# Column quarters for norms and router, softmax ahead of the tokens' transposes, and a regrouped first block

## The chip, the cores and the metric

The kernel runs on one core of a Trainium2 chip. The metric is the device time of one execution in microseconds (us). TensorE (PE) multiplies, VectorE (DVE) and ScalarE (ACT) work elementwise, GpSimd (POOL) does a little, and SyncE (SP) starts the DMAs. All arithmetic is float32; a matmul of 128x128 weights by 512 columns stands in the trace as two records.

## The reference

Two blocks of two layers each on a sequence of 512 tokens and width 1024. The second block takes 256 context tokens beside them. Shortened:

```python
def first_block(x, mem, ...):
    for l in range(2):
        h = rms_norm(x, norm_mix_w[l])
        x = x + hybrid_mixer(h, ...)     # sliding window, "fox" (forgetting) attention, SSM of 16 heads; then w_out
        x = x + memory_cross_attention(rms_norm(x, ...), rms_norm(mem, ...), ...)
    return rms_norm(x, final_norm_w)

# forgetting attention: c = cumsum(log_f)
logits = q @ k * scale + c[query] - c[key]
# SSM: per head, y = (C B^T * decay) @ (x * dt) + C @ state * exp(acs)

def second_block(x, c, ctx, ...):
    for l in range(2):
        m = silu(c) @ w_mod[l] + b_mod[l]           # six shifts, scales and gates
        h = rmsnorm(x) * (1 + m[1]) + m[0]          # the context cx likewise
        x = x + m[2] * (token_mixers(h, hc, ...) @ w_out[l])
        x = x + m[5] * expert_choice_ffn(modulate(rmsnorm(x), m[3], m[4]), ...)
        # the context too in layer 0

def expert_choice_ffn(h, w_router, ...):            # 16 experts
    aff = softmax(h @ w_router)                     # over the experts
    vals, idx = top_k(aff.T, 2 * t // 16)           # 64 tokens (context: 32) for each expert
    ...                                             # gather, gated FFN, weighted scatter
```

## The kernel before, in words

Activations lie transposed: `x` and `h` are eight tiles of 128 channels by up to 768 columns (512 tokens `T`, then 256 of memory or context). Weights come as 748 "units" of 512 KB (`in_stream`) into a ring of eight slots, some into `y_sb`, `h_sb` and `work` during the experts. SP starts the DMA of a slot as soon as PE has counted up `w_turn` for the unit in it. Each engine's program is written out in order; the engines meet by semaphores. On PE `claim(b, who)` waits until bank b's last reader has freed it. Everything that follows stays in the order of the code, so an instruction that waits holds back all behind it on its engine.

- **Norms** (`sum_squares`, L1524): ACT squares two tiles at a time, PE multiplies eight tiles by a matrix of ones (128 columns wide), which leaves the sum on all partitions; ACT takes Ln and Exp (`deviations`), DVE multiplies (`norm`, `modulated`). There are eleven such sums of 512 columns and five of 256.
- **First layer** (`first_layer`, L1622 on PE, L1883 on ACT, L2012 on DVE): norm, ten projections, five multiplications by the rotation matrix `C_ROT1` with DVE work behind each (three operations of 128x512), then `attention` over sliding-window units with projections "beside". After the fifth unit DVE runs `decays`: gates, their cumulative sum, and the negated sum. Then fox attention: each of 16 units has for two halves the scores, two matmuls that add c of the query and take off c of the key (one operand is a broadcast 0/1 column), and the mask.
- **SSM** (from L1649 on PE): twelve convolved projections, transposes of `xbc` that ACT copies out, small matmuls that bring gates and sums to tokens (`tok`), six state products, then the loop over 16 heads. Per head: `broadcast_sums` (bank hh % 2), ACT exponential `e_off`, DVE four `tensor_scalar` of 128 columns, ACT exponential of `diff`, DVE four `scalar_tensor_tensor` (`m_dec`, with the head's dt) and one `tensor_tensor` (`c_off`), PE seven matmuls with 64-column weights (`xs_tok`, `prev`). `pair_out` is two DVE operations per pair of heads.
- **Modulation beside the heads**: three of 48 units per head (`mod_unit`, eight matmuls with 32-column weights in four column groups), 12 groups copied out by ACT, and `mod_columns`: four matmuls of 128x128 weights by 2 columns for each group.
- **Output and memory attention** (L1719 on): projections in two halves with norms between.
- **Second block** (`pe_second`, `act_second`, `dve_second`): norms, projections, grid attention, gated recurrence, output, norm, `experts`.
- **experts**: PE waits for all tiles of `h`, multiplies tokens by the router weights (weights: 128x128 of `h`, 16 columns moving, 48 matmuls with the context), transposes the tokens (12 groups of 4, ACT copies), DVE starts the softmax, ACT's Exp stands behind its twelve copies. Then DVE `choose`: eight rounds of `max` and `match_replace` on 512 columns, and in layer 0 four rounds on 256; a scan gives ranks, PE turns them, DVE builds one-hot matrices, PE gathers.

## Time and profile before

| | us |
|---|---|
| median of 3 runs (lowest to highest) | 3955.86 (3952.66 to 3958.94) |
| the profiled execution's own time | 3957.54 |
| its span in the trace | 3955.8 |
| busy: PE, DVE, ACT, POOL | 3695.8, 1177.2, 909.4, 142.1 |
| HBM read | 404.49 MB, 103 GB/s over the span |

The span is the time from the first to the last instruction of the execution; its own time lies 1.7 us above. Busy time of an engine says little by itself: what matters is which wait ends last in each stage. "PEclk" is the TensorE clock that was granted, as a share of 2.4 GHz; its two levels are 1.0 (2.4 GHz) and 0.5 (1.2 GHz).

### The profile page before, as it was taken

The page shows a single profiled execution, that of the slowest core. Times are in us where ns is not written, and L with a number is a line of the kernel's source. Part 1 is how long each engine was busy: PE and PEld are TensorE (multiplying, and loading weights), DVE is VectorE, ACT ScalarE, POOL GpSimd, SP SyncE. Part 2 cuts the span into 40 slices and gives each one's busy share as a digit, 9 for nine tenths or more (in the row PEclk, how much of TensorE's full clock was granted, in tenths as well). Part 3 has the DMA queues.
Part 4 walks back from the last instruction along what each step waited for, and adds up shares of the span by engine and source line. Part 5 has one row for each costly group of instructions (what it writes and reads, how often), then busy time and mean ns, then how long its engine had stood idle before and what let it go on. Part 6 is the DMA issues. An engine that isn't in the chain of part 4 may idle for free.

```text
span 3955.8 us, 46968 instructions
## 1 busy us (share of the span) xinstructions
PE 3695.8 (93%) x19856; PEld 2170.5 (55%) x19856; DVE 1177.2 (30%) x2568; ACT 909.4 (23%) x1710; POOL 142.1 (4%) x162
## 2 busy tenths in 40 slices
PE   8999899999999899999999889879999999787999
PEld 4555464754465464755756566654434656554553
DVE  1322441021322441022433584120002333752011
ACT  1343220111343220113224220211112233311110
POOL 0000000000000000000000340000000000320000
PEclk9999999999999999999999999889999999887999
DMA  3111261311111271312100001137762110012897
GB/s 141 59 49 48 74 246 64 114 47 64 54 53 47 69 253 64 112 40 92 38 27 33 1 2 56 62 128 281 288 255 86 38 43 22 1 49 101 318 345 278
DMA packets 113104, 409.63 MB, mean 104 GB/s; under 512 B 12289, under 2 KB 14465, under 8 KB 112513
## 3 DMA queue, kind: packets, MB, share of 16 engines
q1 hardware_dynamic: 112896, 406.63, 28.5%
q8 instruction: 159, 2.61, 0.3%
q14 instruction: 49, 0.39, 0.0%
HBM read 404.49 MB, written 2.10 MB: 103 GB/s over the span
## 4 chain that ended last, share of the span: by engine, by line
PE 88%; DVE 8%; ACT 2%; issue 1%; DMA 1%; POOL 0%; DVEq 0%; SPq 0%; ACTq 0%
PE bank L1487 85%; PE bank L1594 1%; DVE work L1275 0%; DMA ring<-in_stream 0%; ACT work L1822 0%; DVE h_sb L2117 0%; DVE work L1345 0%; DVE work L1973 0%; ACT h_sb L892 0%; DVE work L1975 0%; DVE ring L1249 0%; DVE small L1344 0%; DVE levels L1275 0%; DVE ring L1248 0%; PE bank L1655 0%
## 5 line engine op out<-in xcount | busy, mean ns | idle before, releaser
L1487 PE MATMUL bank<-h_sb,ring 128*128 128x512 f32 (+1 forms) x3152 | 1234.9, 545 | 14.9 <-DVE y_sb L1149 4.6
L1487 PEld LDWEIGHTS bank<-h_sb,ring 128*128 128x128 f32 x3152 | 588.4, 191 | 549.7 <-issue 518.4
L1487 PE MATMUL bank<-y_sb,ring 128*128 128x512 f32 (+1 forms) x1152 | 476.2, 576 | 14.1 <-DVEq L196 9.7
L1487 PE MATMUL bank<-work 128*128 128x128 f32 (+5 forms) x3168 | 438.2, 317 | 46.8 <-DVEq L196 15.3
L1487 PEld LDWEIGHTS bank<-work 128*128 128x128 f32 (+2 forms) x3168 | 325.5, 178 | 132.1 <-issue 84.4
L1487 PEld LDWEIGHTS bank<-y_sb,ring 128*128 128x128 f32 x1152 | 220.6, 192 | 265.7 <-issue 247.9
L1487 PE MATMUL bank<-ring,h_sb 128*128 128x128 f32 (+3 forms) x2304 | 317.0, 314 | 18.7 <-ACTq L196 17.2
L1788 ACT ACTIVATE work<-bank 128x512 f32<-128x512 f32 (+1 forms) x275 | 140.2, 525 | 804.0 <-PE bank L1487 634.2
L1487 PEld LDWEIGHTS bank<-ring,h_sb 128*128 128x128 f32 (+2 forms) x2304 | 266.0, 195 | 60.5 <-issue 39.2
L1487 PE MATMUL bank<-ring,work 128*64 128x512 f32 (+1 forms) x800 | 209.3, 596 | 0.8 <-DMA ring<-in_stream 0.8
L1487 PE MATMUL bank<-y_sb,work 128*64 128x128 f32 (+2 forms) x920 | 168.7, 430 | 0.0
L1487 PE MATMUL bank<-work,y_sb 128*128 128x512 f32 (+1 forms) x496 | 137.8, 436 | 13.1 <-DVE ring L1249 6.6
L1799 ACT ACTIVATE h_sb<-x_sb 128x1024 f32<-128x1024 f32 (+1 forms) x56 | 48.0, 896 | 434.5 <-DVEq L196 428.6
L1788 ACT ACTIVATE y_sb<-bank 128x512 f32<-128x512 f32 (+1 forms) x163 | 86.9, 555 | 194.2 <-PE bank L1487 183.2
L1985 DVE TENSOR_REDUCE small<-bank 128x1 f32<-128x256 f32 (+3 forms) x96 | 41.7, 465 | 287.4 <-PE bank L1487 287.2
L1452 POOL MEMSET work<- 128x1024 f32 x4 | 3.7, 951 | 3194.6 <-ACTq L196 3194.6
L1487 PE MATMUL bank<-h_sb,const 128*128 128x512 f32 (+1 forms) x262 | 104.7, 556 | 14.0 <-ACT h_sb L1799 6.0
L1487 PEld LDWEIGHTS bank<-ring,work 128*64 128x64 f32 (+1 forms) x800 | 57.5, 128 | 96.8 <-issue 96.7
L1487 PEld LDWEIGHTS bank<-work,y_sb 128*128 128x128 f32 (+1 forms) x496 | 59.3, 169 | 85.4 <-issue 61.8
L1822 ACT ACTIVATE work<-work,small 128x256 f32<-128x256 f32 (+3 forms) x124 | 73.1, 590 | 128.2 <-DVEq L196 128.1
L1487 PE MATMUL bank<-ring 64*128 64x128 f32 x840 | 78.9, 331 | 23.8 <-DVE work L1275 15.1
L1594 PEld LDWEIGHTS bank<-const,work 128*128 128x128 f32 x576 | 69.0, 141 | 57.0 <-issue 39.4
(274 smaller groups left out, 3543.6 us busy)
## 6 DMA issues: line engine op xcount, KB each, us to landing
ring<-in_stream SPq DMA_DIRECT2D x578, 512.0 KB, 4.4
y_sb<-in_stream SPq DMA_DIRECT2D x110, 512.0 KB, 6.2
h_sb<-in_stream SPq DMA_DIRECT2D x40, 512.0 KB, 8.0
work<-in_stream SPq DMA_DIRECT2D x20, 512.0 KB, 9.7
work<-in_bias SPq DMA_DIRECT2D x2, 2688.0 KB, 9.4
x_sb<-in_xT SPq DMA_DIRECT2D x4, 512.0 KB, 6.1
out<-x_sb SPq DMA_DIRECT2D x8, 256.0 KB, 2.0
const<-in_consts SPq DMA_DIRECT2D x1, 1058.0 KB, 15.8
```

Source lines behind the costliest of these rows:

```text
L1452: ins = V.memset(level_sums[d][n], 0.0)
L1487: return nc.tensor.matmul(o, a, b, start=first, stop=last, skip_group_check=True)
L1594: ins = nc.tensor.transpose(banks[b][:, j * P:(j + 1) * P], scores_in(i - 1, s)[:, kb * P:(kb + 1) * P], ident)
L1788: me.link(A(o, i, func, **kw), freed_by_act, wait=False)
L1799: me.link(A(dst[:, k:k + 2, :], src[:, k:k + 2, :], ACT.Square), squares_ready, wait=False)
L1822: me.link(A(at, banks[s][:, 0:u["nk"]] if raw else at, ACT.Exp, bias=nmax[:, j:j + 1], scale=1.0 if raw else -1.0, accum_out=rsum[:, j:j + ...
L1985: me.link(V.reduce_max(m, banks[s][:, 0:nk], AX.X, negate=True), max_ready, wait=False)
```

## The change

1. Sums of squares: weights of 32 columns of ones, tile k in column group k % 4 (`quarter_squares`), so that four partial sums stand on four groups of 32 partitions. ACT copies them (`quarters`), one more matmul by the full matrix of ones adds them (`add_quarters`), and the scale divides by 32. In the out and memory stages these calls stand between projections.
2. Router: the router's weights (32 columns of the slot) are stationary, `h` moves, in column quarters, each tile as soon as it is ready. ACT copies the parts, six (four) matmuls with `C_EXPERTS` add them token-major. The tokens' transposes are split into groups 0-1, 2-5 and 6-11, around softmax and choosing; ACT's Exp comes after two copies.
3. Choosing: context experts lie on partitions 32 to 47 beside the grid's on 0 to 15, in one `[48, 512]` table filled with -1, so four of the eight rounds choose for both.
4. First layer: the five rotations stand among the projections (banks 4 and 5).
5. Fox: c of the query and of the key are added by one matmul instead of two. `decays` makes the tables for it: two copies, two memsets and four `tensor_scalar` of 128x512 more.
6. SSM: gates and sums go to tokens first; DVE copies `xs_tok` out and multiplies by dt there, `m_dec` becomes one `tensor_tensor` of 512 columns. Three banks for `broadcast_sums`, four buffers for `m_dec` and `c_off`, heads in pairs whose matmuls alternate between the two column halves.
7. Modulation: `mod_columns` (48 matmuls per layer) gives way to `add_mod_rows` (12 matmuls by 512 columns, weights of 32 columns) and four transposes after the output projections' first half.

```diff
-            def sum_squares(b, tile, n, k_tiles=KT, what=C_ONES):
-                claim(b, None)
-                for k in range(k_tiles):
+            def quarter_squares(b, tile, n):
+                claim(b, "act")
+                for k in range(KT):
                     if k % 2 == 0:
                         pe.wait_ge(squares_ready, me.nth(squares_ready))
-                    ins = mm(banks[b][:, 0:n], cst(what), tile(k), k == 0, k == k_tiles - 1)
+                    at = slice(32 * (k % 4), 32 * (k % 4) + 32)
+                    ins = mm(banks[b][at, 0:n], cst(C_ONES, 32), tile(k), k < 4, k >= 4)
                 ins.then_inc(full_for_act, 1)
+            def add_quarters(b, n, at=0):
+                pe.wait_ge(quarters_ready, me.nth(quarters_ready))
+                claim(b, None)
+                mm(banks[b][:, 0:n], cst(C_ONES), quarter_sums[:, at:at + n], True, True).then_inc(full_for_act, 1)
... ACT
+            def quarters(b, n, at=0):
+                bank_full()
+                me.link(A(quarter_sums[:, at:at + n], banks[b][:, 0:n], ACT.Copy), freed_by_act)
+                me.notify(quarters_ready)
... PE, experts
-                for j in range(n_tok):
-                    for k in range(KT):
-                        ins = mm(banks[0][:, j * 16:j * 16 + 16], h[:, k, j * P:(j + 1) * P], w[:, k, 0:16],
-                                 k == 0, k == KT - 1)
+                for s in range(1 + both):
+                    claim(s, "act")
+                    for k in range(KT):
+                        tile_ready()
+                        of = slice(32 * (k % 4), 32 * (k % 4) + 32)
+                        ins = mm(banks[s][of, 0:(T, CTX)[s]], w[:, k, 0:32], h[:, k, SPANS[s]], k < 4, k >= 4)
+                    ins.then_inc(full_for_act, 1)
+                turn_tokens(range(2))
+                pe.wait_ge(freed_by_act, parts_read)
+                claim(2, "dve")
+                for j in range(n_tok):
+                    ins = mm(banks[2][:, j * 16:j * 16 + 16], logit_parts[:, j * P:(j + 1) * P], cst(C_EXPERTS, 16), True, True)
+                ins.then_inc(full_for_dve, 1)
+                turn_tokens(range(2, 6))
... DVE, choose
-                for s, cap in enumerate((CAP, CAP_CTX)[:1 + both]):
-                    for _ in range(cap // 8):
-                        me.link(V.max(top8, left[:, SPANS[s]]))
-                        me.link(V.match_replace(left[:, SPANS[s]], top8, left[:, SPANS[s]], -1.0))
+                for n in range(CAP // 8):
+                    rows = slice(0, 48 if both and n < CAP_CTX // 8 else 16)
+                    me.link(V.max(top8[rows, :], left[rows, :]))
+                    me.link(V.match_replace(left[rows, :], top8[rows, :], left[rows, :], -1.0))
... PE, first_layer
+                    if 2 <= n < 7:
+                        pe.wait_ge(freed_by_act, projected[n - 2])
+                        claim(4 + n % 2, "dve")
+                        mm(banks[4 + n % 2][:, :], cst(C_ROT1), flat((n - 2) * T, T), True, True).then_inc(full_for_dve, 1)
... PE, head loop, modulation
-                def mod_columns(g):
-                    pe.wait_ge(mod_rows_ready, me.nth(mod_rows_ready))
-                    for n in range(4):
-                        ins = mm(banks[7][:, 8 * g + 2 * n:8 * g + 2 * n + 2], mod_rows[:, g % 2, n * P:(n + 1) * P],
-                                 cst(C_PICK, 2), True, True)
+                def add_mod_rows(q):
+                    for _ in range(4):
+                        pe.wait_ge(mod_rows_ready, me.nth(mod_rows_ready))
+                    for j in range(4):
+                        ins = mm(banks[7][32 * j:32 * j + 32, :], cst(C_PICK + 4 - 2 * q, 32), mod_rows[j], q == 0, q == 2)
... fox_units
-                                 (half, 0, n, one.to_broadcast([64, P]), negc[r, 0:n]),
-                                 (half, 0, n, c[r, qi], one.to_broadcast([64, n]))]
+                                 (half, 0, n, decay_of[t][r, qi], decay_keys[r, 0:n])]
... DVE, decays
+                        me.link(V.tensor_copy(decay_all[of_queries, :], decay_all[rows, :]))
+                        me.link(V.memset(decay_all[rows, :], 1.0))
+                    for t in range(4):
+                        me.link(V.tensor_scalar(decay_of[t], decay_all, const[:, C_DECAY + t:C_DECAY + t + 1], None, ALU.mult))
... PE, heads
+                for t in range(HEADS // 2):
+                    for n in range(PER_PAIR):
+                        mod_unit(PER_PAIR * t + n)
+                    for half in range(2):
+                        pe.wait_ge(operand_ready, me.nth(operand_ready))
+                        broadcast_sums(2 * t + half + 3)
...
+                    for c in range(CHUNKS):
+                        for earlier in range(1 + (c > 0)):
+                            for hh in (2 * t, 2 * t + 1):
+                                rows = slice(hh % 2 * 64, hh % 2 * 64 + 64)
...
+                                if earlier:
+                                    ins = mm(banks[b][rows, cs], prev[:, c - 1, hs], c_off[hh % 4][:, cs], False, True)
+                                else:
+                                    ins = mm(banks[b][rows, cs], xs_tok[:, c, hs], m_dec[hh % 4][:, cs], True, c == 0)
...
+                add_mod_rows(2)
... DVE, tokens of the SSM (ACT's copies of xs_tok are gone)
+                for c in range(CHUNKS):
+                    for g in range(2):
+                        bank_full()
+                        me.link(V.tensor_tensor(by_head(xs_tok[:, c, g * T:(g + 1) * T]), by_head(banks[(2 * c + g) % 4][:, :]),
+                                                per_head(tok, c, g), ALU.mult), freed_by_dve, wait=False)
... DVE, heads
-                    for c in range(CHUNKS):
-                        cs = slice(c * P, (c + 1) * P)
-                        me.link(V.scalar_tensor_tensor(out=m_dec[:, r, cs], in0=diff[:, r, cs],
-                                                       scalar=tok[:, c * 16 + hh:c * 16 + hh + 1], in1=cbm[:, g, cs],
-                                                       op0=ALU.mult, op1=ALU.mult), wait=False)
+                    me.link(V.tensor_tensor(m_dec[hh % 4], diff[:, r, :], cbm[:, g, :], ALU.mult), wait=False)
+                    if hh >= 3 and r:
+                        pair_out((hh - 3) // 2)
```

How the order moves, at three places. PE, the norm and the choosing of layer 0 of the second block, from the last output projection to the first gather (`const,h_sb` are the tokens' transposes, `work 128x128` the gather). Before:

```order
L1487 MATMUL bank<-y_sb,ring 128x256 x8
L1487 MATMUL bank<-h_sb,const 128x512 x8
L1487 MATMUL bank<-h_sb,const 128x256 x8
L1487 MATMUL bank<-ring,h_sb 128x16 x48
L649 MATMUL bank<-const,h_sb 128x128 x48
L656 MATMUL bank<-const,small 16x128 x6
L1487 MATMUL bank<-const,work 128x16 x6
L1487 MATMUL bank<-work 128x128 x80
```

Now:

```order
L1518 MATMUL bank<-h_sb,const 32x512 x8
L1518 MATMUL bank<-h_sb,const 32x256 x8
L1518 MATMUL bank<-work,const 128x512
L1518 MATMUL bank<-work,const 128x256
L1518 MATMUL bank<-h_sb,ring 32x512 x8
L1518 MATMUL bank<-h_sb,ring 32x256 x8
L661 MATMUL bank<-const,h_sb 128x128 x8
L1518 MATMUL bank<-const,work 128x16 x6
L661 MATMUL bank<-const,h_sb 128x128 x16
L1518 MATMUL bank<-const,small 16x128 x4
L1518 MATMUL bank<-const,small 32x128 x2
L661 MATMUL bank<-const,h_sb 128x128 x24
```

48 router matmuls of 16 columns became 16 of 512 or 256 columns and six small ones, and 24 of the 48 transposes now come behind the turned affinities.

PE, two heads of the SSM (`ring,cond` modulation units, `work,const` broadcast sums, 64x128 the heads' products). Before, one head, and then the next begins alike:

```order
L1487 MATMUL bank<-work,const 128x512
L1487 MATMUL bank<-const,h_sb 128x2 x4
L1487 MATMUL bank<-ring,cond 32x128 x24
L1487 MATMUL bank<-work 64x128 x2
L1487 MATMUL bank<-work,h_sb 64x128
```

Now, the first pair:

```order
L1518 MATMUL bank<-work,const 128x512 x3
L1518 MATMUL bank<-ring,cond 32x128 x48
L1518 MATMUL bank<-work,const 128x512 x2
L1518 MATMUL bank<-work 64x128 x4
L1518 MATMUL bank<-work,h_sb 64x128 x2
L1518 MATMUL bank<-work 64x128 x2
```

The pair's products stand together, after both heads' operands.

DVE, `decays` between two sliding-window units, now:

```order
L2096 SCALAR_TENSOR_TENSOR work<-work 8x512
L2098 SCALAR_TENSOR_TENSOR work<-work 8x512
L2100 TENSOR_SCALAR work<-work 8x512
L2102 COPY work<-work 8x512
L2103 MEMSET work 8x512
L2105 TENSOR_SCALAR work<-work,const 128x512 x2
L2105 TENSOR_SCALAR levels<-work,const 128x512 x2
L2106 SCALAR_TENSOR_TENSOR work<-work 16x512
```

The first five rows stand twice (rows 0 to 7 and 64 to 71); copy, memset and the four rows of L2105 are new, before the next unit's mask.

## Rows read from the trace of the kernel before

**Rows 1.** Page: busy us of each engine (share of the span); ACT's costliest group, copies

```profile
PE 3695.8 (93%) x19856; PEld 2170.5 (55%) x19856; DVE 1177.2 (30%) x2568; ACT 909.4 (23%) x1710; POOL 142.1 (4%) x162
...
L1788 ACT ACTIVATE work<-bank 128x512 f32<-128x512 f32 (+1 forms) x275 | 140.2, 525 | 804.0 <-PE bank L1487 634.2
```

**Rows 2.** Timeline (start, us, engine, operation, [idle before]): choosing, layers 0 and 1

```profile
2540.99 20.63 PE L1487 MATMUL bank<-ring,h_sb 128*128 128x16 f32 x96 [9.36 <-ACTq L196]
...
2561.46 8.29 PE L649 MATMUL bank<-const,h_sb 128*128 128x128 f32 x48
...
2570.48 0.33 ACT L989 ACTIVATE small<-small 128x96 f32<-128x96 f32 x1
...
2574.12 0.68 DVE L1344 MAX8 small<-work 16x8 f32<-16x512 f32 x1
...
2586.05 0.42 DVE L1344 MAX8 small<-work 16x8 f32<-16x256 f32 x1
...
2593.43 2.73 PE L1487 MATMUL bank<-const,work 16*128 16x16 f32 x12 [20.94 <-DVE work L1351]
...
2598.22 19.64 PE L1487 MATMUL bank<-work 128*128 128x128 f32 x160 [2.06 <-issue]
...
3614.27 13.81 PE L1487 MATMUL bank<-ring,h_sb 128*128 128x16 f32 x64 [7.87 <-ACTq L196]
...
3655.25 16.59 PE L1487 MATMUL bank<-work 128*128 128x128 f32 x128 [1.70 <-issue]
```

**Rows 3.** Timeline: a norm between output projections; PE groups: column-quartered matmuls, all

```profile
594.02 7.03 PE L1487 MATMUL bank<-h_sb,const 128*128 128x512 f32 x16
...
603.28 9.23 PE L1487 MATMUL bank<-y_sb,ring 128*128 128x512 f32 x17 [2.23 <-DVE y_sb L1951]
...
L1487 PE MATMUL bank<-ring,cond 128*32 128x128 f32 x1536 | 49.8, 279 | 0.0
```

**Rows 4.** Stretches (rotations; router): us, busy PE PEld DVE ACT POOL; PEclk; DMA; GB/s

```profile
88.50:101.40 12.90, 4.58 (x12) 1.84 (x12) 10.38 (x15) 1.99 (x3) 0.00 (x0) 0.79 0.00 0
...
2545.00:2555.00 10.00, 10.00 (x48) 10.00 (x49) 0.00 (x0) 0.00 (x0) 0.00 (x0) 0.50 0.73 294
```

**Rows 5.** Heads of the SSM: stretches, timeline, and PE matmuls alternating between column halves

```profile
506.00:559.00 53.00, 48.87 (x697) 37.28 (x698) 35.48 (x101) 16.05 (x28) 0.00 (x0) 1.00 0.85 302
...
1819.00:1822.00 3.00, 2.95 (x7) 1.43 (x8) 2.96 (x6) 3.00 (x6) 0.00 (x0) 1.00 1.03 416
...
507.34 0.38 PE L1487 MATMUL bank<-work,h_sb 128*64 128x128 f32 x2
...
507.65 1.12 PE L1487 MATMUL bank<-work,const 16*128 16x512 f32 x2
...
511.40 1.14 DVE L2126 SCALAR_TENSOR_TENSOR work<-h_sb,small,cpad 128x128 f32<-128x128 f32 x4 [0.77 <-ACT h_sb L1910]
...
512.46 0.68 DVE L2129 TENSOR_TENSOR work<-work,h_sb 128x512 f32<-128x512 f32 x1
...
514.66 1.13 DVE L2117 TENSOR_SCALAR h_sb<-bank,small 128x128 f32<-128x128 f32 x4 [1.52 <-ACT h_sb L1908]
...
L1487 PE MATMUL bank<-y_sb,work 128*64 128x128 f32 x480 | 32.6, 279 | 0.0
```

**Rows 6.** PE groups: matmuls that add c, 0/1 operand stationary; timeline: decays and behind it

```profile
L1487 PE MATMUL bank<-const,work 64*128 64x512 f32 x32 | 8.2, 590 | 0.0
...
L1487 PE MATMUL bank<-const,work 64*128 64x384 f32 x32 | 6.5, 483 | 0.0
...
L1487 PE MATMUL bank<-const,work 64*128 64x256 f32 x32 | 4.8, 377 | 0.0
...
L1487 PE MATMUL bank<-const,work 64*128 64x128 f32 x32 | 3.2, 272 | 0.0
...
159.97 0.48 DVE L2039 TENSOR_SCALAR work<-work,small 16x512 f32<-16x512 f32 x1
...
163.59 0.70 PE L1487 MATMUL bank<-work 64*128 64x256 f32 x4 [1.61 <-DVE small L1980]
```

More of the change, by code:

```diff
@@ L489, in build @@
         hidden_t = [v.rearrange("p (k s) -> p k s", k=4) for v in (rstd[:, 0:512], flat(12032, 512), acc_o[:, 0:512])]
-        aff_t, left, ranks = (work[0:16, 8960 + n * ALL:8960 + (n + 1) * ALL] for n in range(3))
+        logit_parts = flat(7424, ALL)
+        left, ranks = (work[0:48, at:at + T] for at in (9728, 10496))
+        CTX_ROWS = slice(32, 48)
         gathered = [[v.rearrange("p (e k s) -> p e k s", e=2, k=KT) for v in pair]
@@ L1324, in choose @@
             def choose(both):
+                me.link(V.memset(left, -1.0))
                 bank_full()
```

292 lines of the change are left out of this document (156 added, 136 removed).

## The prediction

> **What bounds the kernel now.** I read the page first. TensorE is busy for 3695.8 of the 3955.8 us of the span [rows 1]; the other engines are far below. So the change can save in two ways: less TensorE work where TensorE never rests, and shorter waits in the few stretches where it rests. Then I cut the span into stages and read the timeline where TensorE was idle. The largest such place is the choosing of experts: from the router's first matmul to the first gather it takes 57.2 us in layer 0 and 41.0 us in layer 1 [rows 2]. Others are the rotations, where TensorE works 4.6 of 12.9 us [rows 4], and the norms. In the heads of the SSM TensorE works 48.9 of 53.0 us (five pairs of heads, 10.6 each) while the DMA engines stand at 0.85 and 302 GB/s [rows 5]: two resources close together.
>
> **The change, part by part.** A matmul of 128x128 weights and 512 columns takes 0.88 us (7.03 / 8) [rows 3]. Eight column-quartered ones of 128 columns take 0.52 us: 49.8 us over 96 units [rows 3]. One whole matmul of 128 columns would be a quarter of 0.88, 0.22 us, and eight 1.76 us; so quartering gains a factor 3.4, and eight quartered matmuls by 512 columns cost 8 x 0.88 / 3.4 = 2.1 us.
>
> 1. *Covered norms* (out and memory stages; per layer two of 512 columns, one of 256). Where the first now stands between projections it cost 594.02 to 603.28 = 9.3 us [rows 3], the waits for Ln, Exp and VectorE included. After: 2.1 + 0.9, and the wait lies under the next projection: saves 6.3. The second of 512 saves 7.0 - 3.0 = 4.0, the one of 256 half of it, 2.0. Four transposes for the modulation cost 4 x 0.17 (8.29 / 48 [rows 2]) = 0.7. Per layer 11.6, and about 1.5 for a low clock that no longer follows the rest, an estimate: 13 us; twice, **26**.
> 2. *Norms on the path* (start of each first layer, the first block's final norm, four of the second block). TensorE waits anyway. What counts is the chain behind the last squares: before the rest of eight matmuls, now the last pair (0.5), ACT's copy (0.6 with its start; 0.53 in the mean [rows 1]), one matmul (0.9). Each saves 1.5 to 5 us, the more where 256 columns follow 512. But TensorE idles longer before it begins again, and behind a rest its clock is at the 1.2 GHz level: 0.79 in the mean over the rotations, 0.50 in the router [rows 4]. I take **17** for the seven, between 7 and 25.
> 3. *Rotations.* TensorE's 4.4 us (five by 0.88) stay, now among projections, and the stretch of 12.9 us goes [rows 4]; VectorE's 10.4 us are hidden by projections of 7 us each. Saved 8.5, and some 2.3 because the window units no longer begin at the low clock: 10.8 per layer, **21.6**.
> 4. *Fox.* One of two equal matmuls goes: 8.2 + 6.5 + 4.8 + 3.2 = 22.7 us over both layers [rows 6]. TensorE does not rest in this stage, so all of it is saved: **22.7**.
> 5. *Its price, `decays`.* VectorE gets four operations of 128x512 and four of 8x512 between two window units, at about 0.48 each [rows 6] and with gaps 4.1 us. Behind them waits the next unit's mask, and for that the scores of the unit after on TensorE, which already wait 1.61 us for it [rows 6]; nothing is left to hide more. Per layer -4.1 and -0.9 for the clock: **-10** (between -4 and -14).
> 6. *SSM, before the heads.* Gates to tokens first, then the transposes, whose copies (now VectorE's, 0.68 as `c_off` [rows 5] instead of 0.53) end later: **-2** in all.
> 7. *Heads.* TensorE per pair now: two sums by 512 columns at 1.1 [rows 5], six units at 0.52 = 3.1, fourteen products at 0.136 (32.6 / 240 [rows 5]) = 1.9, together 7.2 us instead of 10.6. VectorE per head: four `tensor_scalar` 1.13, a wait for ScalarE 0.77, `m_dec` 0.68, `c_off` 0.68 [rows 5], 3.3; per pair with `pair_out`, two more of 128x512, 8.1 us. So VectorE sets the pace: 2.5 us less per pair, 20 per layer. The DMA must bring six units, 3.15 MB, per pair: 7.6 us at the 416 GB/s seen elsewhere [rows 5], 8.9 at the 355 that 302 GB/s at a share of 0.85 would make; eight units lie in the ring beforehand. For a DMA nearly as slow I take 17 per layer: **34** (between 12 and 42).
> 8. *Choosing, layer 0.* The router's matmuls (20.6 us) ride on the tiles as they come, 0.5 behind the last; the transposes (8.3) no longer stand before Exp [rows 2]. The path then: 0.5; two copies 1.1; six small matmuls at 0.43 (20.63 / 48) = 2.6; max and subtraction 0.6; from Exp to the first round 3.6 (2570.48 to 2574.12), and 1.0 more because four groups of transposes stand before the turned affinities; eight rounds 11.9 (2574.12 to 2586.05); of the 7.4 up to 2593.43 four context rounds (3.8) and a third of the rest's columns go, 2.5 stay; 4.8 from there to the gather [rows 2]. Sum 28.6 instead of 57.2: **28.6**. That a round on 48 partitions lasts as long as on 16 I assume from the operations of 8x512, 16x512 and 128x512, which hardly differ.
> 9. *Choosing, layer 1.* The same with four token tiles: 0.5 + 0.6 + 1.7 + 0.5 + 3.4 + 1.0 + 11.9 + 2.4 + 3.6 = 25.6 instead of 41.0: **15.4**.
>
> The expert passes stay as they are: twelve units beside the ring's eight are fetched while choosing goes on, 15 us at 416 GB/s. Sum: 26 + 17 + 21.6 + 22.7 - 10 - 2 + 34 + 28.6 + 15.4 = 153.3 us. The profiled execution took 3957.5 us, 1.7 above the median; 3957.5 - 153.3 = **3804**, some 3802 beside a median run.
>
> A rule speaks against parts 1, 7 and 8. Between the start of the last 64-column product (507.34) and that of the next full-width matmul (507.65) lie 0.31 us [rows 5], where products follow each other at 0.22: a change of width costs about 0.1 us, with some 50 such changes added 5 us in all, inside the range. The Trainium skill (TensorEngine Tiling (Array Packing), Tiling Modes, Key Properties) says that a change of tiling mode drains TensorE, and gives no figure; a costly drain would join the second rival.
>
> **The rivals.**
> - *The heads stay as slow as they are*, held by the DMA or by ScalarE's turns. For it: share 0.85, and ScalarE's copies of the modulation between two exponentials. Against: 416 GB/s elsewhere. Part 7 gives 0: 3804 + 34 = 3838.
> - *Quarters do not overlap when 512 columns move.* Then eight cost 7 us again: eleven norms lose 5 us, five 2.5, the routers 13: about 80, so 3884. Against: the factor 3.4 in rows 3, though with 128 columns.
> - *Softmax is not ahead*: Exp or the parts wait behind something else, and half of what parts 8 and 9 promise is lost: 3826.
> - *Slower than before: the clock.* In the router TensorE was busy all the time and yet at 1.2 GHz [rows 4], with matmuls of 16 columns. If the new, lighter mix in heads and norms leaves the clock there and it does not come back in the projections behind, each us of TensorE work at full clock costs one more; it decides from 153 us of such work on. Heads at half clock, 14.4 us per pair instead of 10.6, are 30 more per layer and 17 not saved: 3804 + 94 = 3898. To be slower than before, a further 60 us of projections must run low: from there 4000 and more. The Trainium skill (TensorE: Matmul & The Clock Gate, What's actually happening) says that the throttled state is the default and activity releases it; by that rule the projections bring the clock back.
>
> **How the numbers follow.** Forecast 0.78; heads 0.09; softmax 0.06; quarters 0.04; clock 0.015; other 0.015. The bounds of parts 2, 5 and 7 add up to -36 and +22; not all at once, so 3782 to 3830 for the likeliest case alone. The range takes in the first and third rival: 3775 to 3848. A measurement can tell 0.2%, 8 us, from no change. All cases but the clock lie far below 3948: faster 0.98, same 0.005, slower 0.015.
>
> **What would show it.** In the new profile: some 29 and 26 us from the last router tile to the gather; the head loop at 8.1 us per pair with waits for VectorE; the stretch of 12.9 us gone; a wait of about 5 us on TensorE behind `decays`; column-quartered sums at about 0.26 us each. Wrong if quartered matmuls by 512 columns stand 0.88 apart, if the head loop keeps 10.6, or if the expert passes get longer because their weights come late.

## The result, and the profile after

| | before | changed |
|---|---|---|
| median of 4 runs (lowest to highest), us | 3954.26 (3949.38 to 3958.94) | 3824.52 (3820.65 to 3825.18) |
| the profiled execution: own time, span | 3957.54, 3955.8 | 3824.45, 3821.3 |

The ratio is 0.967, 95% interval 0.9653 to 0.9687. The forecast was 3804, range 3775 to 3848: the range holds the time, the point is 20 us too low. In a later group of runs the changed kernel gave 3821.21 (4 runs), ratio 0.9653 (0.9639 to 0.9666). The interval of every ratio below is about as wide, 5 us to either side; the difference of two runs carries both intervals and is uncertain by some 7 us. A difference smaller than that is read from the traces, stage by stage, or not at all. One of the five executions of experiment 2 took 5180.22 us at a granted clock of 0.67 and is left out of what follows, while all others of a version agree within 0.4%.

The page of the changed kernel, busy times, against [rows 1]:

```profile
PE 3581.4 (94%) x19542; PEld 2060.3 (54%) x19542; DVE 1179.8 (31%) x2497; ACT 911.5 (24%) x1715; POOL 142.1 (4%) x162
```

TensorE is busy for 114.4 us less and the span fell by 134.5, so 20 us of the gain is idle time of TensorE that went. Choosing in layer 0 and a covered norm, PE's timeline (start, duration, engine, line, operation, idle before), against [rows 2, 3]:

```profile
549.80 1.92 PE L1518 MATMUL bank<-h_sb,const 128*32 128x512 f32 x16
551.66 7.13 PE L1518 MATMUL bank<-y_sb,ring 128*128 128x512 f32 x16
558.63 1.02 PE L1518 MATMUL bank<-work,const 128*128 128x512 f32 x2
...
2447.38 8.40 PE L1518 MATMUL bank<-h_sb,ring 128*32 128x512 f32 x32 [2.55 <-ACT h_sb L920]
2455.71 1.09 PE L661 MATMUL bank<-const,h_sb 128*128 128x128 f32 x8
2456.64 1.41 PE L1518 MATMUL bank<-const,work 128*128 128x16 f32 x12
...
2476.68 2.74 PE L1518 MATMUL bank<-const,work 48*128 48x16 f32 x12 [12.89 <-DVE work L1382]
...
2481.49 1.83 PE L1518 MATMUL bank<-work 128*128 128x128 f32 x7 [2.06 <-issue]
```

Eight quartered matmuls by 512 columns last 1.92 us instead of 7.03, and a projection stands between them and the matmul that adds the quarters. From the router's first matmul to the gather it is 34.1 us (2447.38 to 2481.49). The router's 8.40 us of it now run while the tiles of `h` are still being made: the last tile is ready at 2455.06, and from there to the gather it is 26.4 us, where the forecast had 28.6. The window units behind `decays`, same view, against [rows 6]:

```profile
152.97 0.44 PE L1518 MATMUL bank<-work 128*64 128x128 f32 x4
159.31 1.23 PE L1518 MATMUL bank<-work 64*128 64x256 f32 x4 [5.90 <-DVE small L2043]
160.47 5.38 PE L1518 MATMUL bank<-h_sb,ring 128*128 128x512 f32 x8
```

The wait grew from 1.61 to 5.90 us. The eight records behind it (half a projection) take 5.38 us at a mean granted clock of 0.68. The same eight took as long in the kernel before, behind the shorter wait, while in experiment 3 (below), which has that shorter wait too, they take 3.70 (the kernel before, then experiment 3):

```profile
164.22 5.40 PE L1487 MATMUL bank<-h_sb,ring 128*128 128x512 f32 x8
```

```profile
152.97 0.70 PE L1520 MATMUL bank<-work 64*128 64x256 f32 x4 [1.61 <-DVE small L2045]
153.60 3.70 PE L1520 MATMUL bank<-h_sb,ring 128*128 128x512 f32 x8
```

The heads of both layers (us, busy PE, PEld, DVE, ACT, POOL, granted clock, DMA share, GB/s), then VectorE's timeline, against [rows 5]:

```profile
466.60:535.90 69.30, 61.99 (x1050) 41.55 (x1049) 51.20 (x115) 24.98 (x44) 0.00 (x0) 0.90 0.90 341
1315.90:1388.20 72.30, 64.39 (x1050) 42.99 (x1049) 50.96 (x114) 25.01 (x44) 0.00 (x0) 0.87 0.87 332
```

```profile
504.75 1.13 DVE L2193 TENSOR_SCALAR h_sb<-bank,small 128x128 f32<-128x128 f32 x4
...
508.68 0.69 DVE L2186 TENSOR_TENSOR y_sb<-y_sb,work 128x512 f32<-128x512 f32 x1
...
511.23 0.69 DVE L2197 TENSOR_TENSOR work<-h_sb,cpad 128x512 f32<-128x512 f32 x1 [0.69 <-ACT h_sb L1968]
...
512.56 1.13 DVE L2193 TENSOR_SCALAR h_sb<-bank,small 128x128 f32<-128x128 f32 x4
```

VectorE begins the same operation of the next pair 7.81 us later (504.75, 512.56); the forecast said 8.1.

Lengths of the stages, in us per layer (layer 0, layer 1), between the same instructions in each trace. Fox and the rest of the layer came out within 0.1 us of these values in every profile of the same code. The other stages vary from one profile to the next although their code is the same: projections, window units and the stage before the heads by 2 to 3 us, the heads by 5, the second block's body by 3 to 6. So a difference of one or two us in those is read from the mean of several profiles:

| stage (from, to) | before | changed |
|---|---|---|
| projections and rotations (first projection, first mask of the window units) | 85.2, 85.2 | 77.8, 76.6 |
| window units (to the first maximum of the fox units) | 151.7, 151.9 | 154.7, 154.5 |
| fox (to the memset of `cpad`) | 113.9, 113.9 | 105.5, 105.5 |
| convolution, SSM before the heads (to the first broadcast sum) | 110.0, 110.0 | 110.7, 112.9 |
| heads (to the first out projection) | 88.1, 84.9 | 69.3, 72.3 |
| rest of the first-block layer (to the end of its last projection) | 336.0, 336.0 | 323.5, 323.5 |
| second block, its unchanged body (first projection to the last out projection) | 702.3, 561.5 | 705.0, 566.5 |

### The profile page after: what moved, and what is told of

Its sections match the earlier page's. It is cut to its first block, busy times and chain, and to the rows that moved or that the text cites. A ratio compares the mean times of both kernels' runs of the same rounds, so it can differ in the third digit from the quotient of the medians.

```text
span 3821.3 us, 46294 instructions
## 1 busy us (share of the span) xinstructions
PE 3581.4 (94%) x19542; PEld 2060.3 (54%) x19542; DVE 1179.8 (31%) x2497; ACT 911.5 (24%) x1715; POOL 142.1 (4%) x162
## 4 chain that ended last, share of the span: by engine, by line
PE 86%; DVE 8%; ACT 2%; issue 1%; DMA 1%; POOL 0%; DVEq 0%; SPq 0%; ACTq 0%
PE bank L1518 84%; PE bank L1633 1%; DMA ring<-in_stream 1%; DVE work L1307 1%; DVE h_sb L2193 0%; ACT work L1880 0%; DVE ring L1281 0%; DVE work L2036 0%; DVE work L2038 0%; DVE levels L1307 0%; DVE work L1377 0%; PE bank L1705 0%; DVE cpad L1271 0%; DVE small L1376 0%; DVE ring L1280 0%
## 5 line engine op out<-in xcount | busy, mean ns | idle before, releaser
L1518 PE MATMUL bank<-h_sb,ring 128*128 128x512 f32 (+2 forms) x3200 | 1251.2, 548 | 25.1 <-ACT h_sb L920 13.4
L1518 PEld LDWEIGHTS bank<-h_sb,ring 128*128 128x128 f32 (+1 forms) x3200 | 594.2, 191 | 570.0 <-issue 529.3
L1518 PE MATMUL bank<-work 128*128 128x128 f32 (+7 forms) x3168 | 426.2, 322 | 29.8 <-DVE small L2043 12.2
L1518 PEld LDWEIGHTS bank<-work 128*128 128x128 f32 (+2 forms) x3168 | 317.5, 180 | 123.4 <-issue 85.9
L1518 PE MATMUL bank<-ring,h_sb 128*128 128x128 f32 (+2 forms) x2144 | 283.1, 310 | 1.4 <-ACT work L1033 0.7
L1518 PEld LDWEIGHTS bank<-ring,h_sb 128*128 128x128 f32 (+2 forms) x2144 | 231.9, 185 | 43.7 <-issue 40.9
L1518 PEld LDWEIGHTS bank<-work,y_sb 128*128 128x128 f32 (+1 forms) x496 | 59.6, 171 | 85.2 <-issue 61.8
L1633 PEld LDWEIGHTS bank<-const,work 128*128 128x128 f32 x576 | 69.2, 141 | 56.8 <-issue 40.1
L1518 PEld LDWEIGHTS bank<-y_sb,work 128*64 128x64 f32 (+1 forms) x920 | 61.6, 132 | 68.2 <-issue 63.5
```

The source lines that it names most:

```text
L1518: return nc.tensor.matmul(o, a, b, start=first, stop=last, skip_group_check=True)
L1633: ins = nc.tensor.transpose(banks[b][:, j * P:(j + 1) * P], scores_in(i - 1, s)[:, kb * P:(kb + 1) * P], ident)
```

## The experiments

All are edits of the changed kernel; 4, 10 and 11 make two or three at once. Each group of runs had its own runs of the kernel before: 1, 2, 3 and 5 (median before 3959.02); 6, 7 and 8 with a repeated run of the changed kernel (3959.46); 4, 9, 10 and 11 (3956.29). A "slower" or "shorter" below is against the changed kernel, 3824.52 or 3821.21, if nothing else is named.

**1. The burst of `decays` spread.**

```diff
-                    if between is not None and i == 5:
-                        between()
+                    if between is not None and i in (5, 6, 7, 8):
+                        next(between)
```

`decays` becomes a generator that yields behind each of its two gate blocks and behind the four `tensor_scalar`.

> The work of decays is the same, but VectorE does it in four portions behind the window units 5, 6, 7 and 8 and not in one burst of 12.3 us behind unit 5. Theory A (the forecast's part 5: the burst is what TensorE waits for, 5.9 us in the changed kernel's profile, and the low clock after it): each portion is at most 3.7 us and a unit's slack covers most of it, so the wait falls to under 2 us and the low clock after it goes; 3 to 5 us a layer, time 3815 to 3818. Theory B (VectorE has no slack in the window units: the work costs what it lasts wherever it stands): four waits of 1 to 2 us instead of one, time 3822 to 3826.

Measured: 3799.11 (3796.89 to 3805.43), ratio 0.9599 (0.9586 to 0.9612): more than either theory said. PE's timeline at the same place, and the whole window stage:

```profile
153.99 1.07 PE L1518 MATMUL bank<-work 128*64 128x128 f32 x8
154.99 3.70 PE L1518 MATMUL bank<-h_sb,ring 128*128 128x512 f32 x8
```

```profile
96.82:243.35 146.53, 145.63 (x704) 84.11 (x704) 43.24 (x154) 54.29 (x142) 0.00 (x0) 1.00 0.18 62
```

No wait is left and the clock stays at 1.00. The stage is 146.5 us in both layers, 8.1 less than in the changed kernel, twice the expectation: the whole wait and the low clock went, where I had let a part of each stay. So theory A holds, though its time (3815 to 3818) was missed. The two stages are 16.1 us together and the profile is 19.2 shorter; the rest of the 22 to 25 us of the medians lies inside their intervals.

**2. Rotations behind the projections again** (part 3 undone): the five matmuls by `C_ROT1` after `all_read("act")`, on banks 0 to 3.

> The changed kernel with the five rotations back behind the projections (part 3 undone), all else kept. Theory A (part 3 as forecast: 8.5 us for the stretch and 2.3 for the clock of the window units): slower by 21.6, 3846. Theory B (part of that gain was eaten, as the lengths of the stages in the two profiles say: projections and rotations 6.55 us shorter in layer 0 and 7.8 in layer 1): slower by 14 to 15, 3839. In both, TensorE idles some 8 us a layer again behind the last projection.

Measured: 3842.42 (median of four), ratio 0.9705 (0.9691 to 0.9718), 18 to 21 us slower. Its timeline has the old gap:

```profile
86.71 4.56 PE L1518 MATMUL bank<-work,const 128*128 128x512 f32 x10 [0.69 <-ACT y_sb L1840]
98.93 0.80 PE L1518 MATMUL bank<-work 64*128 64x128 f32 x4 [7.67 <-DVEq L199]
```

The stages up to the fox units are 6.6 us longer in layer 0 and 11.9 in layer 1 (84.8 + 154.3 and 87.6 + 155.4). That is 18.5 by the two profiles, and 19.9 against the mean of the seven profiles that share the changed kernel's code up to the fox units (231.1 a layer). It lies between the theories, 21.6 and 14 to 15, nearer to A. That the rotations behind the projections cost the gap is shown; how much of the clock's part belongs to it isn't.

**3. Two decay products again, no tables** (parts 4 and 5 undone).

```diff
-                                 (half, 0, n, decay_of[t][r, qi], decay_keys[r, 0:n])]
+                                 (half, 0, n, one.to_broadcast([64, P]), decay_keys[r, 0:n]),
+                                 (half, 0, n, decay_all[r, qi], one.to_broadcast([64, n]))]
```

> The changed kernel with the two decay products per fox unit back and without the prepared tables (parts 4 and 5 undone). Theory A (forecast: one product is worth 22.7 us over both layers, its preparation costs 10): slower by 12.7, 3837, the fox stage of a layer 11.35 longer and the window stage 5.0 shorter. Theory B (the stage lengths of the two profiles: fox 8.65 in layer 0): the fox stage only 8 to 9 longer, because something else now bounds it a little; the sum slower by 12 to 13 as well, since the window stage loses 2.4.

Measured: 3826.55, ratio 0.9665 (0.9652 to 0.9678), no slower than the changed kernel within the interval. Both theories missed. The fox stage is 113.92 us, so the product is worth 8.4 a layer; the window stage is 148.4, so the tables cost 6.2 of the 154.6; parts 4 and 5 together bring 4.5 us over both layers, not 12.7.

**4. Two decay products, and `decays` spread** (the smaller work of experiment 3 in the four slots of experiment 1).

> The changed kernel with decays spread over four units and with two decay products per fox unit instead of one (no prepared tables). Theory A (one product is worth 8.65 us a layer, as the fox stage shows when it is put back, and the preparation of the tables costs nothing once spread): slower by 17 than the spread version alone, 3816. Theory B (spreading helped by something else than the tables' time): 3799 to 3806 with the smaller work in decays.

Measured: 3817.57, ratio 0.9647 (0.9633 to 0.966). Window stage 146.75, fox stage 113.9. Beside experiment 1 that is 0.2 and 8.4 longer: spread, the tables cost nothing, and the single product keeps all of its 16.9 us. The run is 18.5 us slower than experiment 1, from another group, where theory A said 17.

**5. Sums of squares whole again, at the new places.**

```diff
-                    ins = mm(banks[b][at, 0:n], cst(C_ONES, 32), tile(k), k < 4, k >= 4)
+                    ins = mm(banks[b][:, 0:n], cst(C_ONES), tile(k), k == 0, k == KT - 1)
```

The copy and the added matmul are gone too, and for the last sum of a layer ACT's Ln stands one copy earlier.

> The changed kernel with every sum of squares by eight matmuls of full width again, at the new places in the program, and without the copy and the added matmul (the quartering of parts 1 and 2 undone, their placement kept). Theory A (quarters overlap as forecast, factor 3.4): the covered norms lose 4.0 us for 512 columns and 2.0 for 256, 20 in all, and the seven on the path 1.5 to 5 each, about 17: slower by 30 to 40, 3855 to 3865. Theory B (what helped was the placement; quartered matmuls by 512 columns stand 0.88 apart or the copy and the added matmul give the gain back): within 5 us of 3824.

Measured: 3841.50, ratio 0.9703 (0.969 to 0.9717), 17 to 20 slower: outside both theories, whose bounds were 30 to 40 and 5. PE's timeline:

```profile
547.54 7.03 PE L1518 MATMUL bank<-h_sb,const 128*128 128x512 f32 x16
554.40 13.90 PE L1518 MATMUL bank<-y_sb,ring 128*128 128x512 f32 x32
```

The rest of a first-block layer is 333.4 us, 9.9 longer than with quarters and 2.6 shorter than before: of part 1's 12.5 us a layer the quarters give 9.9, the new places 2.6. On the path, TensorE's gap before the next weights' matmul grows from 7.16 to 9.10 (start of layer 1), 22.20 to 25.73 (final norm and first norm of the second block), 8.53 to 11.94 and 7.98 to 9.85 (behind the second output projections), 81.28 to 83.89 (expert sums and norm of layer 1): 13.4 us. That is 33 in all in the stages that the edit touches, theory A's figure, but the run is only 19.6 longer by its profile. Stages that it doesn't touch were shorter: the second block's body in layer 0 took 699.9 instead of 705.0 us, the heads 5.1 less in both layers together, projections and window units 3.3. Each of these stages varies between profiles of the same code, and here all are at or near their short end; that this is chance isn't shown.

**6. Only half of each modulation unit loaded.** The second half of a unit's room keeps what lay there.

> The changed kernel with only the first half (512 of 1024 columns) of each of the 96 modulation units loaded; the second half of a unit's room keeps what lay there, so the modulation vectors are not those of the reference. Nothing else differs, TensorE does the same matmuls. Theory A (the heads of the SSM are bound by the transfers, in layer 1 more than in layer 0: 0.84 share with four waits for landings there, 0.97 share in layer 0): layer 1's heads from 74.7 us to some 66, layer 0's from 69.1 to 65 or 66, time 3811 to 3815. Theory B (VectorE's turns, 8.1 us a pair, and ScalarE's copies set the pace, the transfers are only close by): 0 to 3 us less, 3821 to 3824.

The changed kernel repeated beside it, which gave 3821.21:

> The changed kernel itself once more, unaltered, as the point from which the other runs of this group are read: 3824 within 0.2% (3817 to 3832).

Measured: 3812.29, ratio 0.9634 (0.9621 to 0.9647).

```profile
465.80:533.50 67.70, 61.50 (x1050) 42.51 (x1049) 51.16 (x115) 25.11 (x44) 0.00 (x0) 0.90 0.61 196
1308.80:1376.50 67.70, 61.50 (x1050) 42.57 (x1049) 51.18 (x115) 25.11 (x44) 0.00 (x0) 0.90 0.62 201
```

The heads take 67.7 us in both layers. In the nine profiles that share the changed kernel's head loop and loads they took 67.5 to 72.3, 70.0 in the mean of 18. So with all transfers the heads are 2.3 us a layer longer on average, and 4.6 in layer 1 of the first profile (69.2 in the repeated run). Of those 4.6, TensorE waited 1.6 directly for landings; its busy time was 2.9 longer, 64.39 against 61.50, at a granted clock of 0.87 instead of 0.90, and whether the transfers brought that isn't shown. The time lies in theory A's range, but the heads of both layers together hold only some 5 of the 8.9 us by which the run is shorter than the repeated one, where A had 12 in the heads: theory A in kind, between the two in size. The rest lies in stages that the edit doesn't touch. (The expectation counts layer 1's heads from 2.4 us earlier than the table, 74.7 for 72.3.)

**7. Eight modulation units ahead of the heads,** one before and between each of the six state products, on banks 5 and 6; five instead of six units a pair are left.

```diff
-        PER_PAIR, MOD_GROUPS = 6, 12
+        MOD_AHEAD, PER_PAIR, MOD_GROUPS = 8, 5, 12
...
+                        mod_unit(2 * c + g + 1)
                         pe.wait_ge(operand_ready, me.nth(operand_ready))
                         claim(1 + g, "dve")
```

> The changed kernel with 8 of the 48 modulation units of a layer computed ahead of the heads, between the state products, where no transfer runs (share 0.00 over 24 us) and TensorE rests 4.4 us; five units a pair are left instead of six, so 32 units instead of 40 must land during the heads. Theory A (transfers bind the heads): layer 1's heads 8 to 10 us shorter, layer 0's 3 to 8, the stage before 0 to 2 longer per layer: 3808 to 3816. Theory B (VectorE and ScalarE set the pace): the heads stay at 65 us or more, and the 4.2 us of matmuls in the stage before cost up to 2 to 3 per layer: 3824 to 3830.

Measured: 3812.06, ratio 0.963 (0.9617 to 0.9644), inside theory A's range. The loads now run in the stage before (DMA share 0.52, 173 GB/s, where it was 0.00):

```profile
466.60:533.10 66.50, 56.58 (x924) 38.74 (x920) 50.61 (x113) 24.74 (x44) 0.00 (x0) 0.92 0.87 315
1309.60:1377.40 67.80, 57.98 (x925) 39.69 (x921) 50.60 (x114) 24.77 (x44) 0.00 (x0) 0.90 0.88 314
447.50:466.60 19.10, 17.82 (x192) 11.29 (x190) 16.11 (x25) 2.68 (x4) 0.00 (x0) 0.95 0.52 173
```

TensorE has 5.4 and 6.4 us less to do in the heads than in the changed kernel's first profile, and they are only 2.7 and 4.4 shorter, less than theory A said, and above 65 us as theory B said: something else sets their floor. Against the mean of the nine profiles the heads are 5.6 us shorter in both layers together, and the stage before them, which now holds the eight units, is 1.3 longer (111.8 and 111.0 against a mean of 110.7). So 4.3 of the 9.2 us of the medians are seen in the stages that the edit touches.

**8. Tokens' transposes all first** (the order of parts 8 and 9 undone).

> The changed kernel with all transposes of the tokens ahead of the logits and of the softmax, as before (the order of parts 8 and 9 undone), all else kept. Theory A (forecast: the transposes then stand on the path to the ranks): 40 more transposes of 0.17 in layer 0 and 24 in layer 1 ahead of the logits, 6.9 and 4.1, less the 1.0 each that the groups now stand ahead of the turned affinities, and Exp behind their copies: slower by 9 to 11, 3834. Theory B (the gain of parts 8 and 9 came from the router's matmuls alone, and the transposes were hidden either way): within 3 us, 3824.

Measured: 3828.84, ratio 0.967 (0.9657 to 0.9683), 7.6 slower than the repeated run.

```profile
2447.87 5.46 PE L661 MATMUL bank<-const,h_sb 128*128 128x128 f32 x48
2453.17 1.41 PE L1515 MATMUL bank<-const,work 128*128 128x16 f32 x12
```

Router to gather takes 39.2 us instead of 34.1 in layer 0 and 31.6 instead of 29.0 in layer 1. Theory A's mechanism, but 7.7 us where it had 9 to 11, since a transpose lasts 0.11 us here (5.46 / 48) and not the 0.17 of [rows 2], at the full clock instead of the low one.

**9. The context's rounds apart.** The rounds of the context's experts stand for themselves again: four `max` and `match_replace` rounds on rows 32 to 47 behind the grid's eight. I wrote them over the table's full 512 columns, not the 256 that the expectation names.

> The changed kernel with the context's experts chosen in rounds of their own behind the grid's (the part of 8 on the 48 partitions undone; layer 0 alone has a context). Theory A (forecast: a round on 48 partitions lasts as long as on 16, so the four context rounds of 256 columns are saved whole): 3.8 us longer from router to gather in layer 0, time 3825. Theory B (48 partitions made the grid's rounds longer, or the ranks wait for the transposes anyway): under 1 us longer, 3821 to 3822.

Measured: 3828.09, ratio 0.9668 (0.9655 to 0.9682), 4 to 7 slower. VectorE's rounds last 0.69 + 0.08 + 0.67 on 48 partitions and 0.68 + 0.08 + 0.66 on 16 in the changed kernel, so the assumption of part 8 holds. Between the first `max` and the ranks' matmul lie 20.4 us instead of 14.4: four rounds of 1.5.

**10. Spread `decays` and eight units ahead, together.**

> The two edits that made the changed kernel faster, together: decays in four portions and 8 modulation units ahead of the heads. Theory A (the stall behind decays and the transfers in the heads are separate losses, in other stages): the gains add up, 9 from the units ahead and 17 to 22 from the spread decays, from 3821 to 3790 to 3795. Theory B (both only moved the same DMA-bound or low-clock time): the second adds under 4 us, 3797 or more.

Measured: 3797.60 (3797.39 to 3802.62), ratio 0.9599 (0.9585 to 0.9612): the fastest median, 0.6% below the changed kernel. It misses theory A's range by 3 us and lies in theory B's, though not for B's reason: the two edits act in different stages. The window units take 146.5 us in both layers, the whole gain of experiment 1, and beside experiment 7 the profile is 17.5 us shorter. It is the units ahead that bring little. The heads take 67.8 and 68.1, 4.0 less than the mean of the nine profiles in both layers together, but the stage before them takes 111.9 and 112.3, 2.7 more than its mean: 1.3 us are left, and the medians of experiments 1 and 10, from different groups, differ by 1.5 (their ratios not at all). This profile is 6.2 us shorter than experiment 1's, but 2.0 of that is an earlier first projection, 2.8 the heads and the stage before them, and the rest lies in stages that neither edit touches.

**11. The same, with the product of each pair's output with its gate left out.**

```diff
-                    me.link(V.tensor_tensor(y[:, 8 + t, :], y[:, 8 + t, :], gtmp, ALU.mult))
```

> Decays spread and 8 modulation units ahead, and in the heads VectorE's product of each pair's output with its gate (one operation of 128x512 a pair) left out, so that the SSM's half of y holds the gates alone. Theory A (with the transfers out of the way VectorE's turns set the pace of the heads, as the forecast's part 7 has it): 0.68 us less a pair, 5 to 6 a layer, 10 to 12 below the version with the gate: 3781 to 3784. Theory B (TensorE or ScalarE's row copies set the pace): 0 to 3 us less, 3789 to 3794.

Measured: 3798.90 (3789.23 to 3799.18), ratio 0.9593 (0.9578 to 0.9609): the time can't tell it from experiment 10. The heads can: 63.4 and 64.3 us instead of 67.8 and 68.1.

```profile
494.46 1.13 DVE L2203 TENSOR_SCALAR h_sb<-bank,small 128x128 f32<-128x128 f32 x4
...
501.54 1.13 DVE L2203 TENSOR_SCALAR h_sb<-bank,small 128x128 f32<-128x128 f32 x4
```

A pair takes 7.08 us instead of 7.81, 0.73 less, as VectorE lost one operation of 0.69. So VectorE's turns with ScalarE set the pace of such a pair; per layer 4 of the 5.8 us come through. The gain is hidden in the sum: the first projection began 0.9 us later in this run, the projections of both layers took 4.0 more (77.7 twice, against 74.9 and 76.6), and the second block's body took 4.3 more in layer 0 (706.1 against 701.8).

## Why the prediction was right, and where 20 us went

The time came out inside the range, and the waits and overlaps that the parts name are found in the traces. But the point was 20 us off in a range 73 wide: two sizes were worked out wrongly (parts 4 and 2), and about half of the miss lies in stages that the forecast left at nothing. The parts, forecast and by the stages of the two profiles, split by an experiment where one separates them:

| part | forecast | measured | from |
|---|---|---|---|
| 1 covered norms | 26 | 25.0 | rest of the layer, 2 x 12.5 |
| 2 norms on the path | 17 | 14.4 | TensorE's gaps: -0.4, 1.9, 3.5, 3.2, 4.3, 1.9; the 3.2 and the last by when the last tile of `h` is ready |
| 3 rotations | 21.6 | 24.3 | experiment 3 against before, up to the fox units |
| 4 fox | 22.7 | 16.9 | 2 x (113.91 - 105.48) |
| 5 `decays` | -10 | -12.3 | window stages of the changed kernel against experiment 3 |
| 6 before the heads | -2 | -3.6 | stage table |
| 7 heads | 34 | 31.5 | 18.9 + 12.6 |
| 8 choosing, layer 0 | 28.6 | 31.2 | end of the out projections to the gather, 77.1 - 42.7, less 3.2 of part 2 |
| 9 choosing, layer 1 | 15.4 | 16.8 | the same, less 1.9 |
| unchanged second block; first projections; the rest | 0 | -9.7 | 705.0 - 702.3, 566.5 - 561.5; 1.7 against experiment 3; 0.3 |
| sum | 153.3 | 134.5 | the spans: 134.5 |

That the sum fits the spans says nothing for the split, since the stages cover the whole span. No run undid parts 6 and 7. What the pairs of heads, the single operation for `m_dec` and `add_mod_rows` each brought isn't shown.

**Part 3** came out 2.7 above its point. The projections are 8.8 us a layer shorter (76.3 and 76.4 in experiment 3, 85.2 before), the window units 3.3; of these, 1.7 is the half projection behind `decays`, 5.40 before and 3.70 in experiment 3. Undone alone, with the burst of `decays` in place, the part is worth only 18.5 to 19.9 (experiment 2), which suggests that its clock's share depends on what else holds TensorE up in the stage.

**Part 4** failed in its working. I read the worth of one product as the busy time of its groups [rows 6]. Busy time runs to the end of the last matmul, which overlaps the next group. What counts is the distance between starts. The trace of before, PE's timeline in one fox unit:

```profile
270.86 1.13 PE L1487 MATMUL bank<-work 64*128 64x512 f32 x4
271.82 1.02 PE L1487 MATMUL bank<-work,const 64*128 64x512 f32 x4
272.68 1.03 PE L1487 MATMUL bank<-const,work 64*128 64x512 f32 x4
273.64 0.71 PE L1487 MATMUL bank<-const 128*128 128x128 f32 x4
```

The second row lasts 1.02 us and the third starts 0.86 behind it. The other three sizes stand at 0.64, 0.43 and 0.22 (264.59 to 265.23, 258.58 to 259.01, 279.29 to 279.51); a unit of each is 2.15 us, and four of each are 8.6 a layer. Experiments 3 and 4 found 8.4. The reading was open to me before the prediction.

**Part 5** named the right place and the right wait. Its bounds (-4 to -14) hold the result near their end. The wait grew by 4.3 us in layer 0 and 4.6 in layer 1, where I had 4.1; the low clock behind it costs 2.2 and 1.6 against experiment 3, where I had 0.9. Against the kernel before, that low clock is nothing new, as its row of 5.40 shows: the table books it as gained in part 3 and lost again in part 5. And the statement "nothing is left to hide more" was true only of the place: experiment 1 shows that the same work costs nothing once no unit carries more than its slack.

**Part 2** is 2.6 below its point and inside its bounds of 7 to 25. The chain behind the last pair of squares was sized at 0.5 + 0.6 + 0.9 us. At the start of layer 1 PE's timeline of the changed kernel shows 1.05 + 0.79 + 1.10, and the stretch beneath it has the full clock:

```profile
861.34 1.05 PE L1518 MATMUL bank<-h_sb,const 128*32 128x512 f32 x4 [0.16 <-ACT h_sb L1851]
863.18 1.10 PE L1518 MATMUL bank<-work,const 128*128 128x512 f32 x2 [0.79 <-ACTq L199]
866.50 4.08 PE L1518 MATMUL bank<-h_sb,ring 128*128 128x512 f32 x5 [2.22 <-DVE h_sb L2014]
```

```profile
861.34:864.28 2.94, 2.15 (x6) 0.44 (x6) 0.00 (x0) 0.60 (x1) 0.00 (x0) 1.00 0.00 0
```

So the clock is not what was missed. I had taken the 0.5 and the 0.9 from long rows of matmuls, divided by their number; a pair or a single one that something waits for lasts to its own end, 1.05 and 1.10 us. It is the error of part 4 the other way round. The norm ahead of the router in layer 0 shows what the part is worth where 256 columns follow 512, PE's start of the sums and ScalarE's last tile (before, then changed):

```profile
2521.15 10.48 PE L1487 MATMUL bank<-h_sb,const 128*128 128x512 f32 x32
2540.10 0.49 ACT L889 ACTIVATE h_sb<-h_sb,small 128x256 f32<-128x256 f32 x1
```

```profile
2438.78 4.57 PE L1518 MATMUL bank<-h_sb,const 128*32 128x512 f32 x32
2454.57 0.49 ACT L917 ACTIVATE h_sb<-h_sb,small 128x256 f32<-128x256 f32 x1
```

The last tile is ready 19.44 us behind the start of the sums before and 16.28 now; with whole sums (experiment 5) it is 19.44 again. And the first norm, which I had among the seven, gained nothing: its first projection started at 17.98 instead of 17.62, and between 16.8 and 18.9 in the profiles of the experiments.

**Part 6** is -3.6 by the first profile alone, in whose layer 1 the stage took 112.9 us. The ten profiles with this stage's code have 110.7 in the mean, 0.8 a layer more than before, so the forecast of -2 is nearer than the table says.

**Part 7** was right by its own mechanism. VectorE's pace is 7.81 a pair (forecast 8.1), shown by experiment 11, and with all transfers the heads are 2.3 us a layer longer in the mean, shown by experiment 6. What the forecast left out is `add_mod_rows`: VectorE's turns last 3.15 us within a pair, but one turn took 6.54 in layer 0 (498.21 to 504.75) and one 7.70 in layer 1, both where TensorE has the four wide matmuls of `add_mod_rows` before the next sums. The two such turns of a layer take 4.38 and 4.56 in experiment 6, 2.6 us a layer more than 3.15 each, even with half the loads. That these matmuls are what lengthens the turns was read from their place and not tried. The rival "heads stay as slow" fell.

**Parts 8 and 9** gave 4 us more than forecast: the transposes and small matmuls run at the full clock now (0.11 us a transpose where I took 0.17, the six that add the router's parts 1.41 where I took 2.6). Before, they stood behind 20.6 us of router matmuls at a granted clock of 0.50; now they stand behind 8.40 us of wide ones at 0.80. The rivals on quarters and softmax fell: 1.92 us for eight matmuls, Exp at 2458.81 with two copies ahead of it.

**The rest** is what I had at nothing, and the largest miss. The second block's code is the same, yet its body took 8 us more. In layer 0 it took 699.9 to 706.1 in the 13 profiles of the changed kernel and its edits, on either side of before's 702.3, so the 2.7 us there are within what it varies by. In layer 1 it took 566.5 to 569.5 in all 13, before's single profile 561.5. The stretch from the end of the recurrence on shows it:

```profile
3425.00:3599.00 174.00, 151.29 (x1094) 97.86 (x1092) 88.97 (x171) 30.23 (x52) 35.15 (x45) 0.91 0.13 46
```

```profile
3305.00:3482.00 177.00, 154.30 (x1090) 100.47 (x1089) 89.17 (x171) 30.23 (x52) 35.15 (x45) 0.88 0.13 45
```

(before above, changed below). The work and the waits are alike, the granted clock is 0.03 lower, and all 3.0 us by which the stretch is longer are busy time of TensorE (154.30 - 151.29). Why it comes out so, and whether the kernel before would show it in another profile, wasn't tried and stays open: about half of the 20 us has no shown cause. The clock rival, far larger, fell: 0.968 over the whole span.

## What to carry to other kernels

The worth of a matmul group on a full TensorE is the distance from its start to the next start, not its busy time; for one that something waits for it is the time to its end. Work that a slack-rich engine does between units should be cut to the slack of one unit: the same VectorE operations cost 16 us more in one burst than in four portions. Work moved ahead of a stage must be charged to the stage that takes it up: of 4.0 us gained in the heads 2.7 went there. Where many parts change at once, compare lengths between like instructions in several profiles: some stages repeated within 0.1 us, others moved by 5 with the same code, and a single pair of profiles can't tell which.

## What was not expected of the hardware

The same first projections, with the same waits, took 74.9, about 76.5 or 77.8 us in different runs of identical code. The rows of two runs (experiment 10, then the changed kernel) show it, timeline first, then the stretch with its clock:

```profile
16.92 13.97 PE L1521 MATMUL bank<-h_sb,ring 128*128 128x512 f32 x32 [2.33 <-DVE h_sb L2022]
```

```profile
17.98 16.93 PE L1518 MATMUL bank<-h_sb,ring 128*128 128x512 f32 x32 [2.33 <-DVE h_sb L2014]
```

```profile
16.92:30.73 13.81, 13.81 (x33) 6.15 (x34) 4.49 (x7) 0.60 (x1) 0.00 (x0) 1.00 0.77 287
```

```profile
17.98:34.75 16.77, 16.77 (x33) 7.26 (x34) 4.49 (x7) 0.60 (x1) 0.00 (x0) 0.82 0.59 216
```

Over the same matmuls the granted clock is 1.00 in the one run and 0.82 in the other, after the same rest of 2.33 us. And VectorE's rounds take the same time on 16 and on 48 partitions within 0.02 us, so two tables laid side by side on partitions are searched for the price of one.
